# The low part of h^T for the projections of layers 0 and 1: written to a second buffer instead of over h^T

## The reference, cut to what matters

```
h = rms_norm(x, g_pre_mix[l]) * (1.0 + sc_m) + sh_m      # 256 x 1024
proj = h @ w_in[l]                                       # 1024 x 3656, float32
mq, mk, mv, dq, dk, dv, qi, ki, wi = jnp.split(proj, offs, axis=-1)
```

## Time and profile before

| | |
|---|---|
| median of 3 runs | 2493.44 us (2492.97 to 2497.28) |
| span of the profiled execution, first to last instruction | 2491.3 us |
| what the median has beyond that span | 2.1 us |
| PE busy | 2374.8 us, 95% |
| DVE busy | 1711.8 us, 69% |
| ACT busy | 1232.0 us, 49% |
| moved by DMA | 650.06 MB, mean 261 GB/s |

### The profile page before, as it was taken

How to read it: one execution, slowest core, us unless ns; L and a number is a source line. 1 busy time by engine, 2 the same in 40 slices (tenths; PEclk the granted TensorE clock), 3 DMA queues, 4 the chain that set the end, 5 groups by cost and what they waited for, 6 DMA issues and landing times. The chain is left out here.

```text
span 2491.3 us, 38197 instructions
## 1 busy us (share of the span) xinstructions
PE 2374.8 (95%) x15277; PEld 1960.9 (79%) x15277; DVE 1711.8 (69%) x1994; ACT 1232.0 (49%) x1317; POOL 651.5 (26%) x349
## 2 busy tenths in 40 slices
PE   6999999899899998999998899999999999999996
PEld 4875999785899774999876578888888888888774
DVE  2575677474876775765586587878787878786556
ACT  2334543443534232333213366677767676766552
POOL 0000000000950352950073223232323232323122
PEclk9999999899999999999999899999999999999998
DMA  9897865467785585685433398999999999998771
GB/s 338 272 349 240 262 210 168 148 197 250 253 259 178 166 282 180 221 266 174 157 114 102 120 356 318 363 353 364 351 359 355 360 355 359 355 361 313 266 273 68
DMA packets 416380, 650.06 MB, mean 261 GB/s; under 512 B 37018, under 2 KB 255222, under 8 KB 416246
## 3 DMA queue, kind: packets, MB, share of 16 engines
q1 hardware_dynamic: 389040, 633.12, 73.8%
q10 hardware_dynamic: 27206, 15.03, 2.2%
HBM read 647.06 MB, written 1.05 MB: 260 GB/s over the span
## 5 line engine op out<-in xcount | busy, mean ns | idle before, releaser
L1611 ACT ACTIVATE region_part<-ring 128x2048 fp32r<-128x2048 f32 x412 | 770.3, 1909 | 276.5 <-PE bank L886 190.6
L2643 DVE TENSOR_TENSOR ring_part<-ring,region_part 128x2048 fp32r<-128x2048 f32 x240 | 569.9, 2404 | 58.8 <-PE bank L1220 32.9
L886 PE MATMUL bank<-ring_part,region_part 128*128 128x512 f32 x1480 | 578.7, 391 | 0.0
L884 PE MATMUL bank<-region_part 128*128 128x512 f32 x1288 | 511.8, 397 | 5.1 <-DVE region L2688 2.2
L885 PE MATMUL bank<-region_part 128*128 128x512 f32 x1152 | 449.7, 390 | 0.0
L1500 POOL TENSOR_TENSOR ring_part<-ring,region_part 128x2048 fp32r<-128x2048 f32 x48 | 248.3, 5180 | 509.4 <-ACT region_part L1611 422.8
L884 PE MATMUL bank<-xn_part,region_part 128*128 128x256 f32 x1152 | 326.6, 284 | 12.3 <-DVE hT_part L2240 10.2
L886 PEld LDWEIGHTS bank<-ring_part,region_part 128*128 128x128 f32 x1480 | 278.2, 188 | 59.5
L886 PE MATMUL bank<-hT_part,region_part 128*128 128x256 f32 x1152 | 324.8, 282 | 0.0
L885 PE MATMUL bank<-xn_part,ring_part 128*128 128x256 f32 x1152 | 324.5, 282 | 0.0
L2195 DVE TENSOR_TENSOR ring_part<-ring,region_part 128x2048 fp32r<-128x2048 f32 x72 | 174.5, 2431 | 178.2 <-ACT region_part L1611 178.2
(11 more groups left out here) (384 smaller groups left out, 3914.2 us busy)
## 6 DMA issues: line engine op xcount, KB each, us to landing
ring<-in_moe_w_gate SPq DMA_DIRECT2D x112, 1024.0 KB, 5.1
ring<-in_moe_w_up SPq DMA_DIRECT2D x112, 1024.0 KB, 5.2
ring<-in_moe_w_down SPq DMA_DIRECT2D x112, 1024.0 KB, 5.0
ring<-in_w_ada SPq DMA_DIRECT2D x48, 1024.0 KB, 9.9
ring<-in_mod_w SPq DMA_DIRECT2D x48, 1024.0 KB, 7.1
ring<-in_w_in SPq DMA_DIRECT2D x44, 1024.0 KB, 5.6
ring<-in_w_up_act SPq DMA_DIRECT2D x22, 1024.0 KB, 5.5
ring<-in_w_up_lin SPq DMA_DIRECT2D x22, 1024.0 KB, 6.1
```

The lines of the kernel that those rows point to most:

```text
L884: nc.tensor.matmul(o, split(a_hi), split(b_hi), start=start, stop=False, skip_group_check=True)
L886: return nc.tensor.matmul(o, split(a_hi), split(b_lo), start=False, stop=stop, skip_group_check=True)
L1611: return nc.scalar.activation(out_, in_, func, **kw).then_inc(*done(*event))
L2643: v.tensor_tensor(split(w), w, whole(hi), ALU.subtract).then_inc(*done("moe_lo", j, e))
```

## The change

The low part of `hT` goes to parts 1 and 2 of `qk`, seen as one buffer of 8 blocks (`hT_low`). `hT` itself stays as it is. Nothing then reads or writes what the whole products need, so the wait for the third whole product goes, and the four subtractions stand at i = 0, ahead of the first `in_low`, behind the waits for `hT_hi` alone. The middle product reads `hT_low`. Layers 2 and 3 and all feed-forward parts are as before.

```
@@ buffers @@
     w_hi = [low("", n=SLOT), low("", n=SLOT), high("", n=SLOT), high("", n=SLOT)]
+    hT_low = qk[:, 1:3].rearrange("p b c s -> p (b c) s")
@@ TensorE, in_tokens_split @@
-                        m = product(o[:, t, :], hT_hi[:, k, ts], hT[:, k, ts], wh[:, k, :], w[:, k, :], k == 0, k == KD - 1)
+                        m = product(o[:, t, :], hT_hi[:, k, ts], hT_low[:, k, ts], wh[:, k, :], w[:, k, :], k == 0, k == KD - 1)
@@ VectorE @@
                     for i, n in enumerate(PROJ_ORDER):
-                        if i == IN_WHOLE - 1:
-                            dve.wait_ge(*until("pe_tile", "in", l, n))
+                        if i == 0:
                             for b in range(4):
                                 dve.wait_ge(*until("hT_hi", l, "in", b))
-                                h = hT[:, 2 * b:2 * b + 2, :]
-                                v.tensor_tensor(split(h), h, whole(hT_hi[:, 2 * b:2 * b + 2, :]), ALU.subtract).then_inc(*done("hT_lo", l, "in", b))
+                                bs = slice(2 * b, 2 * b + 2)
+                                v.tensor_tensor(split(hT_low[:, bs, :]), hT[:, bs, :], whole(hT_hi[:, bs, :]), ALU.subtract).then_inc(*done("hT_lo", l, "in", b))
                         if IN_WHOLE <= i + 2 < len(PROJ_ORDER):
                             in_low(l, PROJ_ORDER[i + 2])
```

## The result

The changed kernel takes 2483.57 us (median of 4 runs, 2482.50 to 2484.22) against 2495.36 us for the kernel before, with one run more than the three shown above (2492.97 to 2498.25). The ratio is 0.995, 95% interval 0.9937 to 0.9964. The forecast was 2483.7 us, range 2480 to 2489. Run once more beside two other kernels it took 2484.91 us (5 runs, 2482.17 to 2488.36) against 2495.09, ratio 0.9966 (0.9952 to 0.9979). The profiled spans are 2481.2 and 2491.3 us; 2481.5 was forecast. So the gain is 11.8 us by the first medians, 10.2 us by the second and 10.1 us by the spans, where 9.75 was forecast; 1.9 of the 11.8 us come from the fourth run of the kernel before, which moved its median from 2493.44 to 2495.36.

A forecast was written before the change was run, and what follows sets the result against it. PE, busy 95%, was taken as the bound, gaining only where it stands still or runs slowly. Pauses of 5.80 us plus slow spells of 3.95 make 9.75: 2493.44 - 9.75 = 2483.7 us, range 2480 to 2489.

The forecast's parts named there:

- The pause: PE's wait for DVE's subtractions before the fourth chunk in layers 0 and 1 goes: 2.90 us each, 5.80 us.
- The slow spells: Half-clock spells in the fourth chunk behind each pause go too: 2.37 us in layer 0, 1.58 in layer 1, together 3.95.
- Layer by layer: The gain split by layer: 2.90 + 2.37 us in layer 0, 2.90 + 1.58 us in layer 1.
- What is late next: At the fifth chunk, weights' low parts come before PE asks, 2.1 and 1.0 us ahead even if they don't move.
- The later work shifts unchanged: All work behind the two changed stretches moves earlier by the full 9.75 us, nothing lost or gained on the way.
- My own range: About 2480 to 2487 us for the full sum; one slow spell avoided or met elsewhere is worth 1.6 to 2.4 us.
- The transfers: Rival: DMA landings at layer 0's last chunk don't move, layer 0 keeps 1.41 us; gain 5.89, time 2487.6, chance 0.10.
- Line 885's reading of both operands from `region`: Rival: the middle product slows at 256 matmuls; 38 ns each eats the gain, 58 ns gives 2498.4 us; chance 0.05.
- the clock comes back elsewhere: Rival: the pause goes but an equal slow spell turns up elsewhere; gain 5.80 us, time 2487.6, chance 0.13.
- the full sum: Main case: pauses and slow spells of layers 0 and 1 all go, 9.75 us, time 2483.7; chance 0.65.

The follow-up runs named there:

- filled pause: The kernel before, with 24 extra matmuls filling each pause of PE ahead of the wait for `hT_lo`; 2492.03 us against 2494.64, ratio 0.9991.
- layer 1 alone: The kernel before with the change made in layer 1 only, layer 0 keeping its old wait and place; 2494.68 us against 2494.22, ratio 0.9995.
- old place, no wait: The kernel before with the second buffer and no wait for the third whole product, subtractions still at i = 2; 2486.94 us against 2494.22, ratio 0.9971.

## Why the prediction was right, point by point

The forecast time, 2483.7 us, was met within 0.2 us, and that closely by luck: the runs of the changed kernel scatter over 6 us, and its median beside the other two kernels was 1.3 us higher. What was right is the mechanism and the size of its terms, which the stretches show.

*The pause, 2.90 us a layer.* Right. Its cause is shown by three runs: with the wait kept and the buffer in use it stands at 2.9 us, without the wait at the old place it is gone but for 0.55 us, and with another wait in its stead it comes back, 2.43 and 1.60 us long.

*The slow spells, 2.37 and 1.58 us.* Right, and right in size: 8.25 - 5.83 = 2.42 us in layer 0, and with the pause filled instead of removed 2.62 and 1.72 us. That the clock fell because PE stood still, and not because of the kind of work at this place, is shown by the filled pause. Why equal pauses of 2.9 us were followed by spells that differ in length, 5.20 and 3.60 us, the runs don't show; in layer 1 the clock fell only about 1.1 us after PE had begun again (470.30 and 471.40).

*Layer by layer.* From the start of the whole products to the first `w_ada` product after the fifth chunk it was 75.02 - 37.72 = 37.30 us and is 69.56 - 37.81 = 31.75: 5.55 us where 5.27 was forecast. Layer 1's stretch is 4.66 us shorter where 4.48 was forecast. Most of the rest is overlap: without the pause the fourth chunk starts 0.20 us before the last whole product ends, in both layers (56.89 against 57.09, 462.59 against 462.79), and the forecast had it start at the end.

*What is late next: nothing.* Right. The fifth chunk started at 63.72 (63.87 forecast), the fifteenth at 139.36 (139.6).

*The later work shifts unchanged.* Right for the work, wrong for the clock, and the difference happened to be small in this profile. Layer 1's first projections lost 6.71 - 5.66 = 1.05 us to a slow spell that reached further into them; later stretches gave back 0.8 us. In the run with layer 1 alone the same kind of loss took the whole gain. My own range allowed for one such spell; that run shows two together, 4.2 us in layer 2.

*The rivals.* The transfers did not bind: the last landing moved 6.45 us. Line 885's reading of both operands from `region` costs nothing: the fifth chunk takes 5.84 us from start to start where it took 5.88, and in the windows of layer 1 from 475 to 535 us, by line and shape (count, busy us, mean ns), before and after:

```profile
L885 PE MATMUL bank<-region_part,hT_part 128*128 128x256 f32 x108 | 30.4, 281 | 0.0
```

```profile
L886 PE MATMUL bank<-region_part 128*128 128x256 f32 x96 | 27.0, 282 | 0.0
```

That the clock comes back elsewhere was given as a rival to the full sum. It is no alternative to it but something that comes on top in some runs: it came true in part in old place, no wait and, in the profiled run, whole in layer 1 alone. On this the Trainium skill (TensorE: Matmul & The Clock Gate, Part 1: The HAM clock gate), which says that one kernel's slow matmuls differ from run to run, agrees with the two groups of runs of the kernel with layer 1 alone (mean granted clock 0.977 to 0.979 and 0.975).

## What to carry to other kernels

An in-place step must wait for every reader of the old value; where a buffer is idle at that time, writing there takes the step out of that chain, and where none is, putting first those products that don't need its result hides most of it, here 2.2 of 2.9 us. A pause of PE costs its own length and can cost the slow clock behind it too, here 2.9 + 2.4 and 2.9 + 1.6 us, so price both; the pauses of 0.55 to 1.60 us in front of the fourth chunks cost only themselves. When a change is worth 0.2 to 0.5%, compare the changed stretch in the profile and many runs: medians of a few runs hold slow spells that lie far from the change.

## What was not expected of the hardware

The granted clock at places far from a change can differ between two kernels whose work there is the same. Behind the same two pauses of 1.8 and 2.2 us in layer 2 it was 1.00 in one kernel's profile and 0.58 and 0.57 in another's. The runs of the kernel with layer 1 alone fall into two groups some 4 us apart, with mean clocks that differ. What decides it at such a place no run shows. In front of the fourth chunks, pauses of 0.55, 0.73 and 1.60 us were followed by full clock, and those of 2.43 to 2.93 us by half clock, without exception in thirteen profiles. Adding matmuls that nobody needs, in time that PE would have stood still, made the stretches around them shorter: by 4.3 us in the two of one experiment and by 3.7 in that of another; the medians point the same way, with intervals that reach to no difference.
